# A convolution group on GpSimd, attention copies on ScalarE, and row work spread anew in a one-core decoder layer

## What is computed

```python
def hybrid_mixer(x, ...):
    h = x @ w_in              # q,k,v,f | swa q,k,v | pool | conv | 4 gates
    y_fox  = forgetting_attention(...)      # 8 heads, causal, over all keys
    y_swa  = sliding_window_gqa(...)        # window 128, sinks
    y_pool = multiscale_pool(...)
    y_conv = silu(layer_norm(depthwise_conv_31(a * sigmoid(g)) + b))   # 512 channels
    merged = sum(sigmoid(gate_b) * (y_b @ p_b) for b in range(4))
    return merged @ w_out
x = layer_norm(ALPHA * x + hybrid_mixer(x))
# PEER, per token and head: the 16 best of 128 x 128 key pairs
act = gelu(einsum('cd,ced->ce', xb, u_tab[idx]))        # 128 experts a token
ffn = einsum('ce,ced->cd', g * act, v_tab[idx])
x = layer_norm(ALPHA * x + ffn)
```

## Time and profile before

| | |
|---|---|
| median of 3 runs | 3703.0 us (3701.93 to 3706.59) |
| the profiled execution | 3718.67 us, its span 3716.9 us |
| mean granted TensorE clock | 0.919 |
| busy | PE 3175.3, DVE 2672.2, POOL 1574.0, ACT 836.4 us |
| DMA | 1073.17 MB, mean 289 GB/s |
| stages of group A with the scores | 0 to 500 us |
| project, attention, merge of group B | 500 to 843, 843 to 1479, 1479 to 1755 us |
| ffn: scores; blocks of `u`; blocks of `v`; what is left | to 1905; to 2889; to 3604; to 3717 us |

### The profile page before, as it was taken

How to read it: one execution, slowest core, us unless ns; L and a number is a source line. 1 busy time by engine, 2 the same in 40 slices (tenths; PEclk the granted TensorE clock), 3 DMA queues, 4 the chain that set the end, 5 groups by cost and what they waited for, 6 DMA issues and landing times.

```text
span 3716.9 us, 40306 instructions
## 1 busy us (share of the span) xinstructions
PE 3175.3 (85%) x14137; PEld 1748.0 (47%) x14161; DVE 2672.2 (72%) x5156; ACT 836.4 (23%) x2013; POOL 1574.0 (42%) x1321
## 2 busy tenths in 40 slices
PE   7579889987888795884899899898999999889970
PEld 5458545755555563542444344444444444333430
DVE  5755449976777665867778896978947874545779
ACT  6334212122121121210110272653810000000000
POOL 5100001124655434434534343435425667777564
PEclk9779999997889797997999999999999999999995
DMA  8469434356878747985869889989899999999996
GB/s 279 139 235 368 184 130 136 109 162 226 280 269 281 264 169 249 380 319 205 318 265 365 298 303 364 326 323 342 307 387 362 384 379 347 325 342 358 407 410 256
DMA packets 313258, 1073.17 MB, mean 289 GB/s; under 512 B 36704, under 2 KB 62944, under 8 KB 309216
## 3 DMA queue, kind: packets, MB, share of 16 engines
q0 software_dynamic: 170704, 606.75, 45.1%
q1 hardware_dynamic: 101904, 363.16, 26.4%
q10 hardware_dynamic: 40448, 100.68, 7.5%
HBM read 931.52 MB, written 138.94 MB: 288 GB/s over the span
## 4 chain that ended last, share of the span: by engine, by line
PE 17%; DMA 14%; POOL 12%; DVE 5%; issue 4%; ACT 1%; DVEq 0%; ACTq 0%; POOLq 0%
PE ps L1781 13%; DMA rows<-v,expert_ids 6%; POOL rows L133 5%; POOL hidden_sums L1746 4%; POOL turned_rows L133 3%; DMA rows<-u,expert_ids 3%; DMA turned_rows<-u,expert_ids 1%; DMA h_side_kept<-mixer_state 1%; DMA turned_rows<-v,expert_ids 1%; DVE rows L162 1%; PE ps L107 1%; PE ps L109 1%; PE ps L108 1%; DVE row_sums L168 1%; DMA mixer_state<-u_t 1%
## 5 line engine op out<-in xcount | busy, mean ns | idle before, releaser
L133 POOL DMA_INDIRECT rows<-u,expert_ids x477 | 581.7, 1219 | 851.3 <-DVE hidden_sums L162 726.9
L1781 PE MATMUL ps<-turned_rows,mixer_state 128*128 128x512 f32 x2048 | 899.7, 598 | 7.3 <-DMA mixer_state<-u_t 6.6
L133 POOL DMA_INDIRECT rows<-v,expert_ids x527 | 609.6, 1157 | 673.3 <-DVE row_sums L168 513.7
L168 DVE SCALAR_TENSOR_TENSOR row_sums<-rows,hidden_sums,row_sums 128x1024 f32<-128x1024 f32 x518 | 654.4, 1282 | 253.7 <-DMA rows<-v,expert_ids 248.5
L1818 PE MATMUL ps<-shared_64k 128*128 128x512 f32 x1536 | 674.8, 602 | 41.1 <-DVE shared_64k L1945 41.0
L1781 PEld LDWEIGHTS ps<-turned_rows,mixer_state 128*128 128x128 f32 x2048 | 388.1, 192 | 479.4 <-issue 469.3
L1818 PEld LDWEIGHTS ps<-shared_64k 128*128 128x128 f32 x1536 | 295.2, 193 | 420.6 <-issue 420.6
L162 DVE CUSTOM_DVE_ANT_0 rows<-rows,x_first 128x1024 f32<-128x1024 f32 x256 | 305.8, 1221 | 47.1 <-DMA rows<-u,expert_ids 44.8
L107 PE MATMUL ps<-x_hi_t_b,shared_64k 128*128 128x384 f16 x912 | 312.4, 343 | 18.4 <-DMA shared_64k<-w_pairs_kept 17.6
L162 DVE CUSTOM_DVE_ANT_0 rows<-rows,branches 128x1024 f32<-128x1024 f32 x221 | 268.7, 1219 | 73.8 <-DMA rows<-u,expert_ids 71.4
L108 PE MATMUL ps<-x_lo_t_b,shared_64k 128*128 128x384 f16 x912 | 310.9, 341 | 0.0
(11 more groups left out here) (526 smaller groups left out, 4990.3 us busy)
## 6 DMA issues: line engine op xcount, KB each, us to landing
mixer_state<-u_t ACTq DMA_DIRECT2D x128, 512.0 KB, 6.9
shared_64k<-v SPq DMA_DIRECT2D x128, 512.0 KB, 7.2
rows<-strips SPq DMA_DIRECT2D x32, 768.0 KB, 7.1
h_kept<-branches ACTq DMA_DIRECT2D x32, 768.0 KB, 10.5
shared_64k<-weights_kept SPq DMA_DIRECT2D x32, 768.0 KB, 8.9
shared_64k<-h_kept SPq DMA_DIRECT2D x32, 768.0 KB, 12.9
shared_64k<-s_pairs_kept SPq DMA_DIRECT2D x32, 512.0 KB, 6.6
rows<-w_t SPq DMA_DIRECT2D x30, 512.0 KB, 5.6
```

What stands on the lines that cost most here:

```text
L133: nc.gpsimd.indirect_dma_start(row_tile(M, n), None, A["u" if r < NSEL else "v"], bass.IndirectOffsetOnAxis(ap=M["idx"][:, c, e:e + 1], ax ...
L168: nc.vector.scalar_tensor_tensor(acc[:, e % 2, :], src, hid[:, c % 2, e:e + 1], acc[:, e % 2, :], ALU.mult, ALU.add).then_inc(used, 1)
L1781: m = pe.matmul(ps[:, 4 + u % 4, 0:UT], uk[u % 4][:, k, :], x1t[:, k, :], start=k == 0, stop=k == KD - 1)
```

## The change

1. In `project` of group B the fourth channel group of the convolution moves from DVE to POOL: per tap a product into a tile of its own and an addition (the first tap one instruction). POOL waits for the convolution's input, does taps 0 to 10, then three gathers after each tap. DVE has 93 tap instructions in place of 124, and its order is: choice 0, the convolution's input, choice 1, six rows.
2. Rows: 60 in place of 35 in `project`, 220 in place of 257 in `attention`, 90 in place of 92 in `merge` (as `[6, 6, 6, 5, 3, 0]` beside the last six blocks), 56 as before beside the scores, and so 726 in place of 712 from the scores on. In the attention units 3, 4 or 5 rows go by the unit's length.
3. In `attention` all copies of turned probabilities are ACT's, and gate half strips go in all units but the odd ones of the two longest blocks (`bare_unit`): 40 of the 48 units in place of 36, and 12 of the 16 steps behind them in place of all 16.
4. The first two strips of `merge` are loaded at the end of `attention` into a tile of their own.
5. In `project` of group A there are six buffers for split weights in place of three.
6. In `ffn`: `ROWS_U_BLOCK` 3.0 for 2.9, `ROWS_V_BLOCK` 2.4 for 2.1, the third window at block 96 for 86, the choices' spans to fit; the three dense norms go between the last twelve rows; one gelu moves from the end of `merge` to the scores.

```diff
-PROJ_ROWS = spans_of(0, [1] * 35)
-ATT_ROWS = spans_of(PROJ_ROWS[-1][1], [0] + [4] * (N_UNIT_B + 2) + [9] * (GB.nc + 1))
-MERGE_ROWS = spans_of(ATT_ROWS[-1][1], [2] * ITEMS + [5] * GB.nc)
+PROJ_ROWS = spans_of(0, [1] * 6 + [2] * 15 + [2] * 3 + [2] * 6 + [1] * 4 + [1] * 2)
-FILL_STEPS = [s for s in range(N_UNIT_B + 2 + 2 * (GB.nc + 1)) if s >= N_UNIT_B or s % 4 != 3]
+def bare_unit(u):
+    return u < N_UNIT_B and u // 2 % GB.nc >= GB.nc - 2 and u % 2 == 1
+def unit_rows(u):
+    if u >= N_UNIT_B:
+        return 3
+    return 2 if bare_unit(u) else (3, 4, 4, 4, 5, 5)[u // 2 % GB.nc]
+FILL_STEPS = [s for s in range(N_UNIT_B + 2 + 2 * (GB.nc + 1)) if not bare_unit(s)][:FILL]
+ATT_ROWS = spans_of(PROJ_ROWS[-1][1], [0] + [unit_rows(u) for u in range(N_UNIT_B + 2)] + [6] * (GB.nc + 1))
+MERGE_ROWS = spans_of(ATT_ROWS[-1][1], [2] * ITEMS + [6, 6, 6, 5, 3, 0])
...
+        def pool_taps(k):
+            src, w = hc[:, 3, k:k + n], M["dw"][:, 3, k:k + 1]
+            if k == 0:
+                nc.gpsimd.tensor_scalar(cacc[:, 3, :], src, w, cv[:, 0, 3:4], ALU.mult, ALU.add).then_inc(pool_tap, 1)
+            else:
+                pool.wait_ge(pool_tap, k)
+                nc.gpsimd.tensor_scalar(M["tap_product"], src, w, None, ALU.mult).then_inc(pool_mul, 1)
+                pool.wait_ge(pool_mul, k)
+                nc.gpsimd.tensor_tensor(cacc[:, 3, :], cacc[:, 3, :], M["tap_product"], ALU.add).then_inc(pool_tap, 1)
...
-            gather_rows(nc, pool, M, A, 0, R_PROJ + NR)
+            gather_rows(nc, pool, M, A, 0, NR)
+            pool.wait_ge(c_in, NCONST)
+            pool.wait_ge(h_done, 4)
+            at = NR
+            for k in range(CK):
+                pool_taps(k)
+                if k >= 10 and at < R_PROJ - 6:
+                    gather_rows(nc, pool, M, A, at, at + 3)
+                    at += 3
+            gather_rows(nc, pool, M, A, at, R_PROJ + NR)
...
-        pe.wait_ge(tap, 4 * CK)
+        pe.wait_ge(tap, len(dve_taps) * CK)
+        if not g.first:
+            pe.wait_ge(pool_tap, CK)
...
+            for i in range(2):
+                sp.dma_start(M["pair"][i], A["s_pairs"][i][:, :, KD:KD + 4, :]).then_inc(M["first_strips"], 16)
...
-                if a:
-                    if u >= 2:
-                        act.wait_ge(pv, u - 1)
-                    copied(act.activation(pt[u % 2][:, a:a + nblk, :].rearrange("p a b -> p (a b)"),
-                                          bank[:, 0:P * nblk], ACT.Copy), k)
+                if a == 0 and u >= 2:
+                    act.wait_ge(pv, u - 1)
+                copied(act.activation(pt[u % 2][:, a:a + nblk, :].rearrange("p a b -> p (a b)"),
+                                      bank[:, 0:P * nblk], ACT.Copy), k)
...
-WINDOW_AT = [30, 58, 86]
-ROWS_U_BLOCK = 2.9
-ROWS_V_BLOCK = 2.1
-CHOICE_SPAN = {5: (0, 20), 6: (24, 47), 7: (52, 75), 3: (82, 105), 4: (112, 150)}
+WINDOW_AT = [30, 58, 96]
+ROWS_U_BLOCK = 3.0
+ROWS_V_BLOCK = 2.4
+CHOICE_SPAN = {5: (0, 20), 6: (24, 47), 7: (52, 75), 3: (78, 92), 4: (112, 141)}
...
+DENSE_NORM_AT = {NROW - 12 + 4 * _d: _d for _d in range(ND)}
```

91 lines of the change are left out of this document (50 added, 41 removed).

## The result

The changed kernel takes 3787.2 us at the median of four runs (3784.5 to 3793.8) where the kernel before takes 3704.8: a ratio of 1.0225, interval 1.0208 to 1.0243. It is 82 us slower; the prediction had 26 us faster.

What follows compares the result with a forecast made beforehand. Largest loss: a PE, ACT and DVE loop in attention; DVE bounds project, PE u, PE and DMA v. Terms -3 + 45 - 81 - 4 + 7 + 10 + 0 = -26 gave 3677 us, range 3630 to 3722.

Steps and rivals of the forecast that it cites:

- of the idle 54 the 39.8 behind DVE's copy should go: Attention units, group B: PE's wait for DVE's copy vanishes, 14 us idle stay; units -45 us, attention -81.
- second rival: Attention: PE's wait moves from DVE to ACT, whose copies stand behind the exponential; attention -50, total 3708 us; chance 0.12.
- against: Attention, argument against the second rival: DVE's minimum comes before its rows, and DVE has 50 us less to do.
- Project: Project of group B: +45 us (+15 to +75), from added rows, idle time and GpSimd's taps against fewer DVE taps.
- what stands behind pooling: Project B: twelve rows, slowed by gathers between taps, then four last taps (10 us); convolution's sums start at 853, before 811.
- Some 16 taps are done in the 48 us of choice 1: Project B: about 16 POOL taps run beside choice 1, undisturbed; 11 others meet DVE's rows and taps, +25 us.
- The lock: Project B: VectorE and GpSimd share a port pair, the loser fully blocked; each contended tap costs DVE 2.3 us.
- Merge and scores: Merge: -4 us (-8 to 0), the time from issue to landing of the load that PE's first matmul waits for.
- Blocks of `v` and end: Blocks of v +10 us (0 to +20), most of 45 us displaced being only moved; the end 0 (-2 to +2).
- Blocks of `u` and group A: Blocks of u: +7 us (0 to +18) for 14 more rows; project of group A: -3 (-8 to 0).
- four cases: Whole kernel: forecast 3677 us (0.55), lock harmless or hidden 3635 (0.18), second rival 3708 (0.12), slower rival 3738 (0.15).
- slower rival: Whole kernel: POOL blocks DVE fully and gathers fall behind; project +75, attention only -50, +13 elsewhere, 3738 us; chance 0.15.

Runs made afterwards that it cites:

- e5: The kernel before with all attention copies of turned probabilities on ACT, behind the next unit's exponential; ratio 1.0062 to the kernel before.
- e3: The changed kernel with ACT's copies in attention ahead of the next unit's exponential; ratio 1.0053 to the kernel before.
- e6: The kernel before with all attention copies on ACT and ahead of the next unit's exponential; ratio 0.9945 to the kernel before.
- e9: e8 with DVE's old order in project of group B (both choices, six rows, then the convolution's input); ratio 0.9791 to the kernel before.
- e1: The changed kernel with all four channel groups of project B's convolution back on DVE; ratio 1.0106 to the kernel before.
- e2: The changed kernel with GpSimd's tap product written with two operations (times weight, plus 0.0); ratio 1.0167 to the kernel before.
- e10: e8 with 2.4 rows for each block of v in place of 2.1; ratio 0.9865 to the kernel before.
- e8: The changed kernel with the convolution back on DVE, ACT's copies ahead of the exponential, and ffn's numbers and norms as before; ratio 0.9821 to the kernel before.
- e12: e9 with 3.0 rows for each block of u in place of 2.9; ratio 0.9829 to the kernel before.
- e14: e9 with ffn as in the changed kernel, except the dense norms behind the last row; ratio 0.9895 to the kernel before.
- e15: e9 with ffn as in the changed kernel, except old choice spans and third window at block 86; ratio 0.9864 to the kernel before.
- e11: e8 with GpSimd's taps again, two-operation product, seventeen taps before the first gather that waits, then four gathers a tap; ratio 0.9884 to the kernel before.

## Why the prediction was wrong

**The step that failed most is attention's**: "of the idle 54 the 39.8 behind DVE's copy should go". 22.6 us came in place of 81. In the units it was +5.9 in place of -45; behind them, where rows and half strips left, -28.5 in place of -36. In the units the work grew as forecast (busy time times clock 325 us, from 313), but 97 us were lost again, from 103: 50 idle where 14 were forecast, 47 to the clock where 30 were. They were lost by the same chain: rows, minimum, exponential, copy. The prediction had this as its second rival, with the right mechanism and the order on ACT as evidence, and its sign, a wait near 40 us with ACT's name, came (48.5); it gave it 0.12 and still 50 us of gain. Its "against" does not hold: DVE did have 50 us less to do (260 busy in the window, from 309), and the wait stayed, since the five rows of one unit stand ahead of the minimum of the next. e5 shows that the copies' 31 us on DVE were not the bound; e3 and e6 show the place of the copies as the cause.

**Project: right in kind, short in size.** 72.6 in place of 45, at the upper bound. DVE reached the second half of its pooling, the step from which the forecast counted, at 826.0, where 820 was forecast:

```profile
825.98 2.18 DVE L646 SCALAR_TENSOR_TENSOR branches<-ps,chan_sb_b,branches 128x384 f16<-128x384 f32 x4
```

Ahead of the pooling (813.6) eleven taps of GpSimd met DVE's taps and rows, and these took 25 us more than their medians (20.8 on taps, 4.2 on rows), as forecast. That it was eleven is luck: eleven taps, not sixteen, were done beside choice 1, and the other five came after 813.6, among the rows of the pooling. Choice 1, taken as undisturbed, lost 8.4 us. The idle time ahead of choice 1 was 10.7 us (12 forecast), and e9 shows that all of it counts.

The term mis-sized most is what stands behind pooling: 33 us forecast to the sums, 49 measured. The product was taken at "about 1 (no row; 1.6 at most)" and measured 2.2, outside the bound, so three rows take 8.6 us in place of 7 and the last four taps 17 in place of 10; and between the use of row 50 and these taps a tap and three gathers still stood on the queue, 6.5 us that the sum left out. "Some 16 taps are done in the 48 us of choice 1" overlooked that the first gather behind tap 10 waits for a row. Without GpSimd's taps the stage costs 31 us (e1), for the 25 rows and the wait ahead of choice 1; without that wait too, 21 (e9).

**The lock.** The Trainium skill's rule (SBUF — State Buffer, "Who interferes with whom"), by which the loser is fully blocked, holds here for the addition and for the short product. The tap of VectorE that meets one ends 0.8 us after it, about its own time (1.0): at 669.57 behind the addition that ends at 668.76, and in e2 at 663.97 behind the product that ends at 663.15. The long product does not fit: the tap that starts with it at 664.43 ends at 666.16 and the next runs in 1.0 us, while the product goes on to 666.65. So the price, 0.7 us, is the same for both products, and 2.3 us for a whole tap.

**Merge and scores** gave 14.0 in place of 4. The first matmul no longer waits on a load, and PE's first matmul of `ffn` comes 2.6 us after DVE's last norm, where it was 13.2. Two rows and a gelu stood behind that norm before and no longer do; which of them counts was not tested.

**Blocks of `v` and end: right in kind, wrong in size.** 34.3 in place of 10. The stage of `v` alone grew by 71 (10 forecast) and the end shrank by 37 (0 forecast). The working had 45 us of blocks displaced and kept a quarter; the 2.4 rows a block cost 8 us (e10 against e8) to 21 to 27 (e12 against e14 and e15). The rows moved to ffn cost 20 to 25 with the old numbers and 11 to 16 with 3.0 rows a block of `u`, all of it behind the last block of `u`, where the prediction had them beside `u` at +7 (measured +1).

**Blocks of `u` and group A** came within 6 us of the forecast, and the place of the norms is worth 5 at most (e14). The result lies beyond all four cases. The slower rival's sign came true, since `project` grew by more than `attention` shrank; but it (3738, 0.15) had project's full price and still gave attention 50 us, and no case took the losses of `v` in full with it. Of the prediction's own signs of being wrong, `project` ended inside 870 to 920 (913), and `attention` is not under 580 (617). The range's upper end, 3722, was 65 us too low. Its own high bounds, project +75, attention -35, `u` +18 and `v` +20 with nothing elsewhere, would have given +78.

## What to carry to other kernels

When a wait is to be removed by giving an operation to another engine, follow the chain behind it one more step: if the operation stands behind the same late instruction there, the wait only changes its name. Moving three lines on ACT was worth 75 us in attention (e3), where moving the work had been worth nothing (e5). In this kernel GpSimd is no free place for elementwise work beside VectorE: count the taps that run beside VectorE at the price of both, and everything on its queue that stands ahead of the last one. The best version here, e9, is 2.1% under the kernel before (0.9755 to 0.9826), without GpSimd's taps.

## What the runs showed that was not expected

A one-operation multiply by a per-partition weight on GpSimd took 2.2 us for 128 x 768 floats; with a second operation that adds 0.0 it took 0.91. The addition of two tiles took 1.80 us at its shortest.

A choice of VectorE, which is made of over 200 mostly short instructions, takes 47.6 us alone, 51.9 beside eleven taps with the short product, 56.0 beside eleven with the long one and 62.7 beside seventeen with the short one (e11). The loss is not spread over them. Two groups of choice 1, first in the changed kernel and then in e1 (mean ns of one behind the busy time):

```profile
L1531 DVE TENSOR_TENSOR shared_64k<-shared_64k 128x256 f32<-128x256 f32 x16 | 9.2, 646 | 0.1
...
L1452 DVE FIND_INDEX8 shared_64k<-shared_64k 128x8 uint32<-128x128 f32 x16 | 4.5, 284 | 0.0
```

```profile
L1519 DVE TENSOR_TENSOR shared_64k<-shared_64k 128x256 f32<-128x256 f32 x16 | 5.5, 418 | 0.1
...
L1440 DVE FIND_INDEX8 shared_64k<-shared_64k 128x8 uint32<-128x128 f32 x16 | 4.6, 284 | 0.0
```

The instructions with two input tiles (TENSOR_TENSOR) took 20.9 us in all in place of 14.9, and casts 2.7 in place of 0.6. The maxima, the searches for an index and the replacements of a matched value, most of the instructions, took the same time to 0.2 us a kind.

And one turned pair of instructions on ACT took the granted clock of 48 units from 0.87 to 0.95.
